# RWKV preparation with three rotating operand blocks, and delta outputs issued with both scan directions side by side

## The reference, cut to what matters

```python
# RWKV-7, per head: what the preparation feeds
w_log = -softplus(-(w0 + tanh(wd) @ w_up)) - 0.5;  decay = exp(-exp(w_log))
a  = sigmoid(a0 + ad @ a_up)                       # the "rate"
kk = l2norm(k * k_k);  k_dir = k * (1 + (a - 1) * k_a)
state = state * w_t + sa * (kk * a) + v_t * k_t    # sa = -state @ kk
o_t   = state @ r_t
# gated delta rule, per chunk: what the delta outputs compute
v_new = u_i - wk_i @ state
o_i   = q_i @ state + attn_i @ v_new               # only the 8 token chunks need it
state = state * exp(g_last) + k_i.T @ v_new
```

## Time and profile before

| | |
|---|---|
| runs | 4603.88, 4608.47, 4622.59 us |
| profiled execution, its own time | 4600.19 us |
| its span, first to last instruction | 4598.3 us |
| granted PE clock, mean over the span | 0.896 |
| busy, share of the span | PE 81%, PEld 63%, DVE 48%, ACT 14%, POOL 17% |
| RWKV preparation, first DMA issue to the scans' first | 3135.2 to 3624.9 us |
| scans, delta and RWKV | 3624.9 to about 4180 us |

### The profile page before, as it was taken

One profiled execution on the slowest core, in us unless ns is written; L12 is line 12 of the kernel. 1 busy time (PEld: TensorE's weight loads), 2 busy tenths in 40 slices (PEclk: granted clock), 3 DMA queues, 4 the chain that ended last, 5 costly groups with the idle time before them and its releaser, 6 DMA issues. The chain is left out here.

```text
span 4598.3 us, 63964 instructions
## 1 busy us (share of the span) xinstructions
PE 3702.8 (81%) x28084; PEld 2898.0 (63%) x28084; DVE 2209.2 (48%) x2148; ACT 644.3 (14%) x980; POOL 794.1 (17%) x818
## 2 busy tenths in 40 slices
PE   7499999999998893599999999864565377885294
PEld 1277777777877782488788888643454355774183
DVE  0367777733325533554533533466767442214733
ACT  0022222211000001011110100111232012210001
POOL 0001111110000000051033150005737670000000
PEclk9799999999999996799999999876788678886697
DMA  7355555555334333222332334344565886651222
GB/s 259 109 157 147 155 154 150 151 165 159 107 96 137 119 101 137 59 76 81 93 96 86 101 107 122 128 167 130 171 200 158 215 167 165 188 185 39 73 100 110
DMA packets 668281, 611.47 MB, mean 133 GB/s; under 512 B 152592, under 2 KB 569416, under 8 KB 659696
## 3 DMA queue, kind: packets, MB, share of 16 engines
q1 hardware_dynamic: 569744, 435.15, 33.2%
q0 software_dynamic: 21936, 95.56, 6.4%
q10 hardware_dynamic: 76336, 76.83, 5.1%
HBM read 471.67 MB, written 135.82 MB: 132 GB/s over the span
## 5 line engine op out<-in xcount | busy, mean ns | idle before, releaser
L361 PE MATMUL front_ps<-b_hT,front_wb 128*128 128x512 f32 x4224 | 979.5, 392 | 19.2 <-DVE front_wb L351 19.2
L1251 PE MATMUL in_ps<-b_hT,in_wb 128*128 128x512 f32 (+3 forms) x4992 | 956.3, 353 | 10.6 <-DVE in_wb L1238 10.6
L361 PEld LDWEIGHTS front_ps<-b_hT,front_wb 128*128 128x128 f32 x4224 | 789.9, 188 | 200.1 <-DVE front_wb L351 22.4
L1251 PEld LDWEIGHTS in_ps<-b_hT,in_wb 128*128 128x128 f32 (+1 forms) x4992 | 816.1, 188 | 157.5 <-issue 15.2
L1236 DVE CAST in_wb<-in_raw 128x2048 fp32r<-128x2048 f32 (+1 forms) x68 | 82.6, 1215 | 560.4 <-PE in_ps L1251 543.1
L349 DVE CAST front_wb<-front_raw 128x2048 fp32r<-128x2048 f32 x88 | 108.1, 1228 | 434.3 <-PE front_ps L361 425.7
L755 POOL DMA_DIRECT2D front_mwb<-in_w_ada x128 | 101.3, 795 | 804.3 <-PE front_mps L765 801.7
L1086 PE MATMUL wout_ps<-wout_wb,wout_pair 128*128 128x512 f32 x768 | 177.3, 393 | 62.7 <-DVEq L1107 62.0
L1086 PEld LDWEIGHTS wout_ps<-wout_wb,wout_pair 128*128 128x128 f32 x768 | 145.4, 190 | 95.1 <-issue 64.7
L351 DVE TENSOR_TENSOR front_wb<-front_raw,front_wb 128x2048 fp32r<-128x2048 f32 x88 | 201.8, 2293 | 3.0
L1003 PE MATMUL merge_ps<-merge_pair,merge_wb 128*128 128x512 f32 x768 | 176.8, 393 | 22.3 <-DVEq L1021 22.3
(11 more groups left out here) (408 smaller groups left out, 4873.5 us busy)
## 6 DMA issues: line engine op xcount, KB each, us to landing
front_raw<-in_w_in SPq DMA_DIRECT2D x88, 1024.0 KB, 6.6
in_raw<-in_w_in SPq DMA_DIRECT2D x67, 1024.0 KB, 5.6
front_mwb<-in_w_ada POOLq DMA_DIRECT2D x128, 512.0 KB, 5.0
r_scr<-rprep_ob ACTq DMA_DIRECT2D x16, 2694.0 KB, 15.0
scan_rops<-r_scr SPq DMA_DIRECT2D x24, 1796.0 KB, 10.7
mod_wb<-in_w_ada SPq DMA_DIRECT2D x8, 4096.0 KB, 12.6
g_scr<-gprep_ob SPq DMA_DIRECT2D x8, 3474.0 KB, 11.1
wo_raw<-in_w_o SPq DMA_DIRECT2D x16, 1024.0 KB, 5.1
```

The lines of the kernel that those rows point to most:

```text
L361: last = self.nc.tensor.matmul(self.ps[:, n % 2, :], self.wb[:, n % 2, x, kt, :], self.hT[:, y, kt, :], start=kt == term == 0, stop=kt == ...
L1251: last = self.nc.tensor.matmul(self.ps[0:width, n % 3, first:end], self.wb[:, n % 2, x, kt, 0:width], self.hT[:, y, kt, first:end], start= ...
```

## The change

Operand blocks become three, used in turn over the 16 (i, d); a block's store is counted by block (`stored[3]`) in place of by direction. The write of block n = 2i + d then waits for the store of n - 3, where it waited for that of n - 2. POOL's third solve waits for the first eight stores by three counters. `rate` has one buffer per direction, and the ACT gate that fills it waits for the operands of the same direction of the pair before (ACT waited for the pair two before). `sel` holds one pair's selector and is refilled by DVE after each `unit_keys`. In the scan, `outputs` issues per head the two directions' products with the state, then the two with the values, where it finished d = 0 before d = 1.

```diff
-        self.sel = st.sb("sel", [InverseNorms.ROWS, RP, 2, RD])
+        self.sel = st.sb("sel", [InverseNorms.ROWS, 2, RD])
-        self.rate = st.sb("rate", [P, 2, 2, TA])
+        self.rate = st.sb("rate", [P, 2, TA])
-        self.ob = [st.sb(f"ob{d}", [P, NCH, R_COLS]) for d in range(2)]
+        self.obs = [st.sb(f"ob{u}", [P, NCH, R_COLS]) for u in range(3)]
+    def ob(self, i, d):
+        return self.obs[(2 * i + d) % 3]
 def unit_keys(self, dve, i):
         dve.sem_inc(self.s["keyed"], 1)
+        if i + 1 < RP:
+            self.select(dve, i + 1)
 def rate_gate(self, act_e, i, d):
-        if i >= 2:
-            act_e.wait_ge(self.s["ops_ok"], 2 * (i - 1))
+        if i >= 1:
+            act_e.wait_ge(self.s["ops_ok"], 2 * i - 1 + d)
 def operands(self, dve, i, d):
-        if i > 0:
-            dve.wait_ge(self.stored[d], 48 * i)
+        if n >= 3:
+            dve.wait_ge(self.stored[n % 3], 48 * (n // 3))
 def norms(self, pe, i):
+        pe.wait_ge(self.s["sel_ok"], i + 1)
 rwkv_prep, POOL:
                     if batch == 1:
-                        pool.wait_ge(m.stored[d], 48 * RP // 2)
+                        for u in range(3):
+                            pool.wait_ge(m.stored[u], 48 * len(range(u, RP, 3)))
 DeltaScan.outputs:
         for h in range(H):
+            o = [self.po[r, h * GD:(h + 1) * GD] for r in rows]
             for d in range(2):
-                r = slice(64 * d, 64 * d + 64)
-                o = self.po[r, h * GD:(h + 1) * GD]
-                self.nc.tensor.matmul(o, self.chan[:, u, d, H * g + h, C:2 * C], self.state[:, g, d, h, :], start=True, stop=False)
-                last = self.nc.tensor.matmul(o, self.tok[r, u, H * g + h, 0:C], self.y[r, g, h, :], start=False, stop=True)
+                self.nc.tensor.matmul(o[d], self.chan[:, u, d, H * g + h, C:2 * C], self.state[:, g, d, h, :], start=True, stop=False)
+            for d, r in enumerate(rows):
+                last = self.nc.tensor.matmul(o[d], self.tok[r, u, H * g + h, 0:C], self.y[r, g, h, :], start=False, stop=True)
```

More of the change, by code:

```diff
@@ L2243, in start @@
         link(nc.vector.memset(self.reset[:, 0:TA:C], 0.0))
-        self.select(dve)
-        for d in range(2):
-            link(nc.vector.memset(self.ob[d][:, T // C:NCH, self.AR + C:self.AR + 2 * C], 0.0))
+        self.select(dve, 0)
+        for ob in self.obs:
+            link(nc.vector.memset(ob[:, T // C:NCH, self.AR + C:self.AR + 2 * C], 0.0))
         dve.wait_ge(self.s["loaded"], 16 * 6)
@@ L2277, in rate_gate @@
         act_e.wait_ge(self.s["za"], 2 * i + d + 1)
-        if i >= 2:
-            act_e.wait_ge(self.s["ops_ok"], 2 * (i - 1))
-        self.alink(self.nc.scalar.activation(self.rate[:, i % 2, d], self.ps_n[:, 0:TA], ACT.Sigmoid, bias=self.column(2 + d, i)))
+        if i >= 1:
+            act_e.wait_ge(self.s["ops_ok"], 2 * i - 1 + d)
+        self.alink(self.nc.scalar.activation(self.rate[:, d], self.ps_n[:, 0:TA], ACT.Sigmoid, bias=self.column(2 + d, i)))
         act_e.sem_inc(self.s["a_out"], 1)
@@ L2341, in mask @@
         mask = self.k.mask[:, d].rearrange("p j t -> p (j t)").unsqueeze(1).to_broadcast([P, NCH, P])
[L2342 removed]
+        self.tt(self.ob(i, d)[:, :, col:col + P], self.ps_m[:].rearrange("p (c x) -> p c x", x=P), mask)
         dve.sem_inc(self.s["m_out"], 1)
@@ L2373, in norms @@
             pe.wait_ge(self.s["a_out"], 2 * i)
-        self.product(self.sel[:, i].rearrange("p h n -> p (h n)"), self.inv, "norms")
+        self.product(self.sel[:].rearrange("p h n -> p (h n)"), self.inv, "norms")
     def decay_product(self, pe, i, d):
@@ L2449, in finish @@
     def finish(self, act_e):
+        for u in range(3):
+            act_e.wait_ge(self.stored[u], 48 * len(range(u, 2 * RP, 3)))
         for d in range(2):
-            act_e.wait_ge(self.stored[d], 48 * RP)
             act_e.wait_ge(self.bonus_st[d], 16 * RP // 2)
@@ L2661, in outputs @@
             pe.wait_ge(self.s["o_out"], 2 * n)
+        rows = [slice(64 * d, 64 * d + 64) for d in range(2)]
         for h in range(H):
+            o = [self.po[r, h * GD:(h + 1) * GD] for r in rows]
             for d in range(2):
-                r = slice(64 * d, 64 * d + 64)
-                o = self.po[r, h * GD:(h + 1) * GD]
-                self.nc.tensor.matmul(o, self.chan[:, u, d, H * g + h, C:2 * C], self.state[:, g, d, h, :], start=True, stop=False)
-                last = self.nc.tensor.matmul(o, self.tok[r, u, H * g + h, 0:C], self.y[r, g, h, :], start=False, stop=True)
+                self.nc.tensor.matmul(o[d], self.chan[:, u, d, H * g + h, C:2 * C], self.state[:, g, d, h, :], start=True, stop=False)
+            for d, r in enumerate(rows):
+                last = self.nc.tensor.matmul(o[d], self.tok[r, u, H * g + h, 0:C], self.y[r, g, h, :], start=False, stop=True)
         last.then_inc(self.s["o_ok"], 1)
```

21 lines of the change are left out of this document (10 added, 11 removed).

## The result

| | before | after |
|---|---|---|
| median of the runs | 4606.18 us (4 runs, 4599.60 to 4622.59) | 4534.10 us (4 runs, 4532.24 to 4537.94) |
| ratio after / before | | 0.9839, 95% interval 0.9812 to 0.9866 |
| profiled execution | 4600.19 us | 4532.24 us |
| its span, mean PE clock | 4598.3 us, 0.896 | 4530.2 us, 0.898 |

The change makes the kernel 72 us faster by the medians, 68 by the two profiled executions. 4560 us and a range from 4540 were forecast: the time lies 26 us under the forecast and 6 us under the range.

What follows compares the result with a forecast made beforehand. The operand pipeline ended the preparation, some 14 us behind POOL; PE bound scan steps 8 to 11. Preparation 15 plus scan 31.7 (7.4 + 5.8 + 18.5) took 46.7 from 4600.2: 4553.5 us, median 4560, range 4540 to 4586.

Steps and rivals of the forecast that it cites:

- Preparation: Stage before the scans: POOL's solves would end it, scans starting 15 us earlier; bounds 0 and 25 (all relief early).
- Pipeline: Preparation's DVE, PE and ACT chain: 45 us of block waits saved, last `r_scr` store issued near 3567, 25 us of slack.
- Small edits: Single `rate` buffer and `sel` refills in the preparation: no cost, or 2 to 5 us if the pipeline still ended it.
- Outputs: Scan's output products on PE: directions run side by side, a group takes 2.9 us in place of 5.78.
- the bank rule: Outputs on PE: differing row tiles can't share a PSUM bank, so only state products pair, saving about 2 us a group.
- Step 7's wait: PE's scan wait for the first RWKV inverses: SP reaches their loads 7.4 us earlier, until POOL's landing holds it.
- Step 7 itself: Scan step 7, apart from its wait: 5.8 us saved by the faster outputs.
- Steps 8 to 11: Scan steps where PE is the bound: 23.1 us saved by outputs, four fifths taken for stalls, 18.5 us.
- (a): Rival: POOL takes all in the preparation, third solve starting at 3415; preparation 0, scan 32, total 4577; 13%.
- (b): Rival: outputs don't pair fully or PE's instruction supply eats it; scan 12 to 22, preparation 15, about 4576 to 4581; 15%.
- (c): Rival: more than forecast, POOL's solves keep most relief and steps 8 to 11 lose nothing; 24 + 40, 4544; 8%.
- (d): Rival: slower, PE packed tighter in the scan is held at 1.2 GHz; up to 58 us cost, 4666; 4%.

Runs made afterwards that it cites:

- e1: The change with the outputs' old loop, so only blocks, rates and selector: 4573.8 us, ratio 0.9928 to the kernel before.
- e9: The change plus 17 DVE operations, both inputs in SBUF, beside POOL's fourth solve: 4542.3 us in one run, that solve 80.75 us.
- e10: The change plus 17 DVE operations, one input in PSUM, beside POOL's fourth solve: 4535.3 us in one run, that solve 70.59 us.
- e3: The change with POOL's third solve waiting only for the stores of blocks 0 to 6: 4538.0 us, ratio 0.9849 to the kernel before.
- e6: The change with two operand blocks in turn in place of three, other edits kept: 4571.3 us, ratio 0.9912 to the kernel before.
- e4: The change with a group's eight state products issued first, then its eight value products: 4528.3 us, ratio 0.9833 to the kernel before.
- e5: The change with the outputs' old order back in delta steps 4 to 6 only: 4546.5 us, ratio 0.9856 to the kernel before.
- e8: The change with the RWKV scan's first inverse completed later, behind delta step 7: 4539.1 us, ratio 0.9842 to the kernel before.
- e2: The kernel before with only the outputs' new loop: 4570.3 us, ratio 0.9926 to the kernel before.
- e7: The change without POOL's third and fourth solve in the preparation: 4490.5 us in one run, preparation 410.4 us.
- e12: The change with grouped outputs, deferred first RWKV inverse and SP's loads reordered: 4530.2 us, ratio 0.9830 to the kernel before.

## Why the prediction was right or wrong

The limits came as forecast: POOL ends the preparation, the outputs' directions overlap, SP waits for POOL in step 7. The sizes did not, and one of them had its mechanism wrong as well. In the profiled executions the gain was 68.1 us (4598.3 - 4530.2) for 46.7 forecast.

- **Preparation, 15 forecast, 32.1 measured. This is the step that failed.** It was said that POOL ends the stage, and it does. The third solve was put 2.2 us later, at 3401; it starts at 3404.99, and 3400.50 in e1. What failed is the sentence behind it: "The four DMAs and the two solves behind it take 200.1 + 11.3 us, less what POOL gains", with 5.5 for the gain. (The reading under it, that the 200.1 us pass "whatever DVE does", is wrong as well: 10.2 us lie between e9 and e10.) From third load to last write the chain lost 20.9 us: 10.9 in the solves (10.2 of them in the fourth), 8.7 in the two loads, which no longer run beside a store, 1.2 in the write between. The relief was taken as proportional to DVE's silence, "about a sixth". What counts is how many DVE operations with two SBUF inputs fall into the solve (e9, e10): 29 became 15, since in the second half of the last iteration DVE only works out of PSUM, and that half moved under POOL's fourth solve. The DMAs were held fixed, although the stores that run beside POOL's loads were among what the change moves (e3). Term by term, in us:

| | before | forecast | change |
|---|---|---|---|
| third load issued at | 3398.8 | 3401 | 3405.0 |
| from there to the last write's issue | 200.1 | 194.6 | 179.2 |
| from there to the scans' first load | 26.5 | 12.3 | 9.5 |
| scans' first load at | 3625.4 | 3608 | 3593.7 |

- **The bounds of this term, 0 to 25, were too narrow** for the same reason: "all of the relief early" held nothing for the DMAs.
- **Pipeline.** Forecast 45 us earlier to 3567; 3574.05 in the change, 3566.38 in e1, 3566.60 in e3: right within 7. But its slack of 25 us was worked out from a POOL chain that was too long; it is about 7. The sign named for it, a last issue 20 us ahead of POOL's last write, failed: 3574.05 is 10 us ahead of 3584.17.
- **Small edits at nothing**: right (e6).
- **Outputs, 2.9 us a group**: 2.94. The two value products do share a bank at full pace (e4). The "about 2 us" that was named for the bank rule is 1.4 by the row's pair time: 12 pairs of 0.36 us in place of 16.
- **Step 7's wait, 7.4 forecast, 8.1 measured** between the two profiles: right by luck in part. It was read as SP's lateness in the kernel before. Against e1 and e5, where the preparation is as in the change, it is 12 to 13 us. PE's wait came to 20.4 us, where about 25 was named as the sign.
- **Step 7 itself, 5.8: 6.8 measured. Steps 8 to 11, 18.5: 20.1.** Of the 4.6 us that were held back for PE's stalls, 1.6 came after all. But B is 137.1 to 142.9 us over the nine kernels with these outputs, with the clock between 0.87 and 0.93 (0.85 in e8), and the change's own profile is the shortest of them; of the two with the old outputs, e1 has 171.0 and before 164.0. So 20 is good to some 5 us.
- **The rest of the 68.1**, 1 us, is scatter in C, D and ahead of the preparation.
- **The difference between profile and median.** 6.5 us were added for it, from three runs that showed 8.3; with four runs of each it is 6.0 before and 1.9 after. This took 4.6 us of the 26.
- **Rivals.** (a), POOL taking all, is out: third load 3405, not 3415. (b) is out by e2, where the outputs alone bring 34 to 36 us; its total was also added up 5 us too high at one end, since scan 22 and preparation 15 give 4571 or 4572, not 4576. (c), the one on this side, came nearest, with 24 us for the preparation and 40 for the scan (about 32 and 35), and had 8%: it deserved more, since the forecast shortened only the solves of POOL's chain and kept its loads as long as they had been beside stores. (d) is out for the change, where the clock from step 8 on was 0.93 before and after; in the other kernels with new outputs it was 0.85 to 0.92, and in e1 with the old ones 0.87, so the outputs' order alone doesn't decide it.

## What to carry to other kernels

When two engines share a stretch, don't scale the slower one's relief by the other's idle time: count the DVE operations with two SBUF inputs that fall beside a GpSimd loop (here 0.6 us each for 128x768, on both sides), and which of its transfers run beside a large store (up to 5 us for 1.5 MB beside 2.7 MB here). A gain in one chain that ends a stage is only as large as the other chain's distance, and that distance moves with the overlap: recompute both ends after the change. Where matmuls use half of PE's rows or columns, order them so that the halves alternate and shapes change as rarely as possible, and expect part of the gain back as waits elsewhere.

## What the runs showed of the hardware that was not expected

- POOL's two later solves, with their loads and writes, cost the operand pipeline 40 us (e7), as much as its waits for blocks had (its last store is issued 38 us earlier in the change and 45 in e1, of 59.1 us of waits).
- 32 passes into one PSUM bank: 5.8 us with 16 changes of shape and one direction finished before the other, 2.9 with the directions alternating and 8 changes, 2.0 with 2 changes (e4).
- Work put into PE's 20 us wait (e8, e12) was given back behind it: clock 0.69 and 0.77 for 0.92, and longer stalls. Why is open.
- A PSUM operand in place of an SBUF one made the same DVE operation 1.6 times as fast (957 against 1568 ns) beside a busy POOL.
